# Small linears with standing weights and streaming tokens, four modulation rows in another linear, and later sines

## The reference, cut to what matters

```python
# odd layer
qkv, g, a_in, b_in = split_cols(a @ w_in, ODD_SPLITS)      # a_in and b_in: 16 columns each
log_a = -jnp.exp(a_log) * jax.nn.softplus(a_in + dt_bias)
beta = jax.nn.sigmoid(b_in)
# hybrid layer: columns for the indexer's head weights (8) and for the gates of the mLSTM (4 and 4)
IN_SPLITS = (Q_RANK, ATT_WIDTH, ATT_WIDTH, IDX_DIM, N_IDX_HEADS,
             MLSTM_WIDTH, MLSTM_WIDTH, MLSTM_WIDTH, MLSTM_WIDTH, MLSTM_HEADS, MLSTM_HEADS)
cos, sin = jnp.cos(ang), jnp.sin(ang)                      # rotary tables from the positions
```

## Time and profile before

| | |
|---|---|
| time, median of 3 runs | 2228.63 us (2227.8 to 2230.28) |
| the profiled execution | 2229.53 us, span 2227.8 us |
| mean granted clock of TensorE | 0.943 |
| PE busy | 2048.6 us, 92% |
| DVE busy | 1507.7 us, 68% |
| ACT busy | 901.8 us, 40% |
| POOL busy | 140.4 us, 6% |
| HBM read | 320.84 MB, 144 GB/s over the span |

### The profile page before, as it was taken

How to read it: one execution, slowest core, us unless ns; L and a number is a source line. 1 busy time by engine, 2 the same in 40 slices (tenths; PEclk the granted TensorE clock), 3 DMA queues, 4 the chain that set the end, 5 groups by cost and what they waited for, 6 DMA issues and landing times. The chain is left out here.

```text
span 2227.8 us, 40146 instructions
## 1 busy us (share of the span) xinstructions
PE 2048.6 (92%) x16858; PEld 1831.8 (82%) x16858; DVE 1507.7 (68%) x2320; ACT 901.8 (40%) x1338; POOL 140.4 (6%) x231
## 2 busy tenths in 40 slices
PE   6998987999999799899988999798899989988997
PEld 5786865788888588688886999698799979887997
DVE  6866566998676758656646777768666666956454
ACT  3436443222222433322325444546444355554443
POOL 0100000011000011201210000000000000000000
PEclk7999989999999889899998999899899999988999
DMA  8532022455553366100003777343357734323552
GB/s 329 200 125 76 1 95 95 176 184 190 187 187 115 117 227 221 45 3 3 3 21 114 256 276 277 106 145 102 125 207 276 275 111 155 130 95 111 181 183 92
DMA packets 59133, 323.94 MB, mean 145 GB/s; under 512 B 6384, under 2 KB 7536, under 8 KB 32624
## 3 DMA queue, kind: packets, MB, share of 16 engines
q1 hardware_dynamic: 33360, 228.97, 29.2%
q0 software_dynamic: 25344, 92.29, 11.8%
q10 hardware_dynamic: 288, 0.66, 0.1%
HBM read 320.84 MB, written 1.05 MB: 144 GB/s over the span
## 5 line engine op out<-in xcount | busy, mean ns | idle before, releaser
L370 DVE TENSOR_TENSOR w_low<-raw,w_high 128x1024 fp32r<-128x1024 f32 (+1 forms) x408 | 473.4, 1202 | 243.5 <-ACT w_high L362 243.2
L362 ACT ACTIVATE w_high<-raw 128x1024 fp32r<-128x1024 f32 (+1 forms) x408 | 402.5, 1035 | 397.6 <-PE banks L407 389.2
L548 DVE SCALAR_TENSOR_TENSOR mod_rows<-mod_rows,silu_condition 128x1024 f32<-128x1024 f32 x176 | 212.9, 1221 | 14.3 <-DMA mod_rows<-rows_dram 11.7
L405 PE MATMUL banks<-ffn_a_l,w_high 128*128 128x256 f32 x704 | 199.7, 284 | 1.9 <-DVE ffn_hidden L1006 1.9
L406 PE MATMUL banks<-ffn_a_h,w_high 128*128 128x256 f32 x704 | 199.1, 283 | 0.0
L407 PE MATMUL banks<-ffn_a_h,w_low 128*128 128x256 f32 x704 | 199.1, 283 | 0.0
L405 PE MATMUL banks<-mlp_a_l,w_high 128*128 128x512 f32 (+1 forms) x512 | 176.7, 345 | 11.9 <-DVE mlp_a_l L690 7.7
L534 POOL DMA_DIRECT2D mod_rows<-rows_dram x176 | 93.2, 530 | 1368.4 <-DVE mod_rows L548 1152.1
L406 PE MATMUL banks<-mlp_a_h,w_high 128*128 128x512 f32 (+1 forms) x512 | 175.2, 342 | 0.0
L407 PE MATMUL banks<-mlp_a_h,w_low 128*128 128x512 f32 (+1 forms) x512 | 174.9, 342 | 0.0
L405 PE MATMUL banks<-mlp_hidden_l,w_high 128*128 128x512 f32 (+1 forms) x512 | 173.3, 338 | 1.3 <-DVE mlp_hidden_l L1014 1.3
(11 more groups left out here) (598 smaller groups left out, 4876.4 us busy)
## 6 DMA issues: line engine op xcount, KB each, us to landing
raw<-panels_dram SPq DMA_DIRECT2D x204, 1024.0 KB, 4.8
mod_rows<-rows_dram POOLq DMA_DIRECT2D x176, 512.0 KB, 5.1
mod_0a_rows<-rows_dram SPq DMA_DIRECT2D x8, 1024.0 KB, 19.4
x_features<-x_features_dram SPq DMA_DIRECT2D x1, 2048.0 KB, 11.3
constants<-small_dram SPq DMA_DIRECT2D x1, 1672.5 KB, 6.8
silu_condition<-conditions_dram SPq DMA_DIRECT2D x2, 512.0 KB, 12.5
out_dram<-x_features SPq DMA_DIRECT2D x4, 256.0 KB, 2.1
constants<-small_dram SPq DMA_DIRECT2D x1, 736.5 KB, 5.4
```

Of the source, the lines that this page charges most:

```text
L362: self.nc.scalar.activation(self.wh[:, m % 2, cols], self.raw[:, slot, cols], ACT.Copy).then_inc(self.w_high, 1)
L370: self.nc.vector.tensor_tensor(self.wl[:, m % 2, cols], self.raw[:, slot, cols], self.wh[:, m % 2, cols].bitcast(F32), ALU.subtract).then_ ...
L405: self.nc.tensor.matmul(out, sh(k), ml(k), start=(opens and k == 0), stop=False)
L548: nc.vector.scalar_tensor_tensor(row if v == nv - 1 else self.scratch[:], row, 1.0, self.cond[v][:], ALU.mult, ALU.mult, accum_out=mod[:, ...
```

## The change

It does five things.

1. `odd_ab_in` becomes one block: the 32 weight columns are stationary (`narrow`) and all 512 tokens stream, 24 products into one bank of 32 partitions. ACT copies it to `pre[0:32, 7, :]`. At panel 1 of `odd_v` PE transposes it in four pieces into bank 7 (`turn_narrow`), and the gate inputs read it from there.
2. `mix_small_in` of both hybrid layers does the same with 256 tokens: 24 products, an ACT copy to `work`, two transposes at panel 0 of `mix_v_in` behind the rotation products, and an ACT copy to `sm`.
3. The gates of the hybrid layers move: the 4 small DVE operations behind the rotary work at `mix_v_in` panel 0, exp and ln to panel 1 behind the relus, the last two DVE operations to the first panel of `mix_rest`.
4. The two Sin activations move from ahead of `mix_in`'s copies into `mix_small_in`, behind ACT's split of the next panel.
5. The rows: `odd_g` takes 1, 1, 2 and 2 and `odd_ab_in` none (6 where there were 10); `odd_out` takes one per panel. `linear` now carries the free marks of the prior linear's banks on.

```diff
@@ -802,7 +802,8 @@
-            info.update(done=done, taken=taken, bank_free=bank_free)
+            kept = prior["bank_free"] if prior is not None else {}
+            info.update(done=done, taken=taken, bank_free={**kept, **bank_free})
@@ -862,6 +863,22 @@
         return product
+
+    def narrow(self, high, low, n, width, nk):
+
+        def product(q, m, bank):
+            return self.product3(bank[0:width, 0:n],
+                                 lambda k: self.wh[:, m % 2, k * width:(k + 1) * width],
+                                 lambda k: self.wl[:, m % 2, k * width:(k + 1) * width],
+                                 lambda k: high[:, k, 0:n], lambda k: low[:, k, 0:n], nk)
+        return product
+
+    def turn_narrow(self, pe, src, out, width):
+
+        for i in range(src.shape[1] // P):
+            last = self.nc.tensor.transpose(out[:, i * width:(i + 1) * width], src[:, i * P:(i + 1) * P],
+                                            self.c("ident")[0:width, 0:width])
+        return last
@@ -1719,7 +1736,7 @@
-    ab = pr.sb("odd_ab", [P, 4, 32], ctx=inner)
+    ab = ps[:, 7, 0:P].rearrange("p (i n) -> p i n", n=32)
@@ -1746,10 +1763,16 @@
                         pr.copy_out(lambda q: gate[:, q, :]), a_ready, info=g_info, rising=True,
-                        beside=lambda which, eng, p: beside(which, eng, 2))
-    ab_ready = pr.linear("odd_ab_in", 1, 4, 4, pr.tokens(high, low, 4, 32, KD),
-                         pr.copy_out(lambda q: ab[:, q, :]), [], prior=g_info, info=ab_info,
-                         beside=lambda which, eng, p: beside(which, eng, 2))
+                        beside=lambda which, eng, p: beside(which, eng, 1 + p // 2))
+    ab_ready = pr.linear("odd_ab_in", 1, 1, 1, pr.narrow(high, low, N, 32, KD),
+                         lambda q, which, eng, bank: nc.scalar.activation(pre[0:32, 7, :], bank[0:32, :], ACT.Copy), [],
+                         engines=("act",), prior=g_info, info=ab_info)
+    ab_turned = pr.sem("odd_ab_turned")
+
+    def turn_ab(pe):
+        for w in ab_ready:
+            pe.wait_ge(*w)
+        pr.turn_narrow(pe, pre[0:32, 7, :], ps[:, 7, 0:P], 32).then_inc(ab_turned, 1)
@@ -1769,8 +1792,7 @@
-        for w in ab_ready:
-            dve.wait_ge(*w)
+        dve.wait_ge(ab_turned, 1)
@@ -1818,7 +1840,8 @@
-    gate_steps = {("dve", 1): gate_inputs, ("act", 1): gate_logs, ("dve", 2): log_decays}
+    gate_steps = {("dve", 1): gate_inputs, ("act", 1): gate_logs, ("dve", 2): log_decays,
+                  ("pe", 1): turn_ab}
@@ -2524,12 +2547,11 @@
-        @pr.block.scalar
-        def _(act):
-            act.wait_ge(angles_ready, 2)
-            nc.scalar.activation(sin[:], sin[:], ACT.Sin).then_inc(ready, 1)
-            nc.scalar.activation(cos[:], cos[:], ACT.Sin).then_inc(ready, 1)
-    return [(ready, 2)]
+    def sines(act):
+        act.wait_ge(angles_ready, 2)
+        nc.scalar.activation(sin[:], sin[:], ACT.Sin).then_inc(ready, 1)
+        nc.scalar.activation(cos[:], cos[:], ACT.Sin).then_inc(ready, 1)
+    return sines, [(ready, 2)]
@@ -2656,21 +2678,23 @@
               engines=who[:8], rising=True, beside=beside_first, info=a_info, first_out=conv_first(0))
-    pr.linear("mix_small_in", 1, 2, 2, pr.tokens(high, low, 2, 32, KD), pr.copy_out(lambda q: sm[:, q, :]), [],
-              engines=("act",), prior=a_info, info=sm_info)
-
-    def beside_q(which, eng, p):
-        if which == "dve":
-            eng.wait_ge(*sm_info["taken"][1])
-            b = lambda name: spread(c(name)[:, 4 * l:4 * l + 4], 1, 2)
-            nc.vector.tensor_tensor(ig, sm[:, :, 8:12], b("b_ig"), ALU.add)
-            nc.vector.tensor_scalar(w_idx[:], sm[:, :, 0:8], (8 * 64) ** -0.5, None, ALU.mult)
-            ch.then(eng, nc.vector.tensor_tensor(lf, sm[:, :, 12:16], b("b_fg"), ALU.add))
-            nc.vector.scalar_tensor_tensor(tmp, lf, -1.0, lf, ALU.mult, ALU.max).then_inc(gates_abs, 1)
+    sm_t = work[0:32, 0, :]
+    pr.linear("mix_small_in", 1, 1, 1, pr.narrow(high, low, N, 32, KD),
+              lambda q, which, eng, bank: nc.scalar.activation(sm_t, bank[0:32, 0:N], ACT.Copy), [],
+              engines=("act",), prior=a_info, info=sm_info,
+              beside=lambda which, eng, p: sines(eng) if which == "act" else None)
+    sm_turned, sm_out = pr.sem("mix_small_turned"), pr.sem("mix_small_tokens")
+
+    def gate_inputs(dve):
+        dve.wait_ge(sm_out, 1)
+        b = lambda name: spread(c(name)[:, 4 * l:4 * l + 4], 1, 2)
+        nc.vector.tensor_tensor(ig, sm[:, :, 8:12], b("b_ig"), ALU.add)
+        nc.vector.tensor_scalar(w_idx[:], sm[:, :, 0:8], (8 * 64) ** -0.5, None, ALU.mult)
+        ch.then(dve, nc.vector.tensor_tensor(lf, sm[:, :, 12:16], b("b_fg"), ALU.add))
+        nc.vector.scalar_tensor_tensor(tmp, lf, -1.0, lf, ALU.mult, ALU.max).then_inc(gates_abs, 1)
     pr.linear("mix_q_up", 1, 8, 8, pr.features(cq_h, cq_l, N, 2, lambda q, k: (q * 2 + k) * P),
-              pr.copy_out(lambda q: qr[:, (q + 4) % 8, :]), [(cq_split, 1)], prior=sm_info, info=q_info,
-              beside=beside_q)
+              pr.copy_out(lambda q: qr[:, (q + 4) % 8, :]), [(cq_split, 1)], prior=sm_info, info=q_info)
@@ -2688,11 +2712,11 @@
             nc.tensor.matmul(ps[:, 6, 0:N], c("rot"), pj[:, KI, :], start=True, stop=True).then_inc(idx_rotated, 1)
+            eng.wait_ge(*sm_info["taken"][0])
+            pr.turn_narrow(eng, sm_t, ps[:, 7, 0:64], 32).then_inc(sm_turned, 1)
         if which == "act" and p == 0:
-            eng.wait_ge(gates_abs, 1)
-            nc.scalar.activation(tmp, tmp, ACT.Exp, scale=-1.0).then_inc(gates_exp, 1)
-            eng.wait_ge(gates_exp, 1)
-            nc.scalar.activation(tmp, tmp, ACT.Ln, bias=1.0).then_inc(gates_log, 1)
+            eng.wait_ge(sm_turned, 1)
+            nc.scalar.activation(flat(sm[:]), ps[:, 7, 0:64], ACT.Copy).then_inc(sm_out, 1)
         if which == "dve" and p == 0:
@@ -2703,8 +2727,10 @@
             nc.vector.tensor_tensor(pj[:, KI, :], pj[:, KI, :], rot[:, 4, :], ALU.add).then_inc(idx_roped, 1)
+            gate_inputs(eng)
         if which == "pe" and p == 1:
             eng.wait_ge(idx_roped, 1)
+            eng.wait_ge(sm_out, 1)
             index_scores(eng, idx_done, range(8), 0, 4)
@@ -2713,10 +2739,10 @@
                                      ACT.Relu).then_inc(idx_relu, 1)
-        if which == "dve" and p == 1:
-            eng.wait_ge(gates_log, 1)
-            ch.then(eng, nc.vector.scalar_tensor_tensor(lf, lf, 0.0, tmp, ALU.min, ALU.subtract))
-            nc.vector.tensor_scalar(nlf, lf, -1.0, None, ALU.mult).then_inc(gates_ready, 1)
+            eng.wait_ge(gates_abs, 1)
+            nc.scalar.activation(tmp, tmp, ACT.Exp, scale=-1.0).then_inc(gates_exp, 1)
+            eng.wait_ge(gates_exp, 1)
+            nc.scalar.activation(tmp, tmp, ACT.Ln, bias=1.0).then_inc(gates_log, 1)
@@ -2778,6 +2804,9 @@
+            eng.wait_ge(gates_log, 1)
+            ch.then(eng, nc.vector.scalar_tensor_tensor(lf, lf, 0.0, tmp, ALU.min, ALU.subtract))
+            nc.vector.tensor_scalar(nlf, lf, -1.0, None, ALU.mult).then_inc(gates_ready, 1)
@@ -3195,17 +3224,19 @@
-            take, _ = pr.row_work("mod2_0a", [(2 * N_MOD, 34, 1, pr.mod2[0], 0, b_mod[0])], slots, [], silu_ready)
+            take, _ = pr.row_work("mod2_0a", [(2 * N_MOD, 30, 1, pr.mod2[0], 0, b_mod[0])], slots, [], silu_ready)
...
+            take_rest, rest = pr.row_work(
+                "mod2_0b", [(2 * N_MOD + 30, 18, 1, pr.mod2[0], 30, b_mod[0]),
+                            (3 * N_MOD, 16, 1, pr.mod2[1], 0, b_mod[1])], slots, [pr.after_rule], [])
...
-                              pr.add_gated(mod, 16, 1, TL), y_split, engines=("dve",), rising=True)
+                              pr.add_gated(mod, 16, 1, TL), y_split, engines=("dve",), rising=True,
+                              beside=lambda which, eng, p: take_rest(eng, 1) if which == "dve" else None)
...
-            ready = mlp(1, mod, 1, TL, ready, lambda t: pr.row_work(
-                "mod2_0b", [(2 * N_MOD + 34, 14, 1, pr.mod2[0], 34, b_mod[0]),
-                            (3 * N_MOD, 16, 1, pr.mod2[1], 0, b_mod[1])], slots, [pr.after_rule], []), {1: 1, 2: 1})
+            ready = mlp(1, mod, 1, TL, ready, lambda t: (take_rest, rest), {1: 1, 2: 1})
...
```

More of the change, by code:

```diff
@@ L2601, in hybrid_mixer @@
     pr.presplit(2)
-    tables_ready = tables()
+    sines, tables_ready = tables()
     tap = lambda b, n: c("conv_w")[:, l * 32 + n * 8 + b:l * 32 + n * 8 + b + 1]
@@ L3229, in second @@
             take = lambda eng, count: None
-            tables = lambda: []
+            tables = lambda: (lambda act: None, [])
             if l == 0:
```

## The result

| | before | after |
|---|---|---|
| time, median (lowest to highest) | 2228.81 us (2227.80 to 2230.28), 4 runs | 2207.26 us (2203.70 to 2210.05), 4 runs |
| profiled execution, span | 2227.8 us | 2206.2 us |
| mean granted clock | 0.943 | 0.951 |

The medians lie 21.6 us apart. The recorded ratio of the times is 0.9894, with a 95% interval of 0.988 to 0.9909, which is 23.6 us less (20.3 to 26.7). The forecast was 2207, 21.6 less. The sum is met, but not each of its terms, and the rest of this document is mostly about two terms that missed in opposite directions.

The account below looks back on a forecast made before the run. PE was taken to bound nearly everywhere (busy 92%). Savings of 13.5 + 3.8 + 1.1 + 3.3 = 21.7 us from 2229.5 gave 2207.8, median 2207; forecast's own bounds 2205 to 2210, with rivals 2202 to 2214 (about 0.8).

Parts of the forecast that it names:

- Part 1: Odd layer's small linear as 24 products of 512 columns: `odd_v` starts earlier, net 13.5 us saved (11 to 14).
- Rival C: Odd layer: fifth or sixth row lands late, DVE splits `odd_v`'s first panel two to three us late; 2210, chance 0.13.
- rival B: Half clock behind the 32-column stationaries in the odd layer and hybrids, as behind the 32-wide products; 2212, chance 0.10.
- The four moved rows: Rows moved to `odd_out`, one per panel, cost nothing; up to 4 x 1.3 = 5 us if the cover were gone.
- Part 2: First hybrid layer: moving the sines removes PE's 2.11 us hole before the rotation and its half clock; 3.8 us saved (2.0 to 4.0).
- Part 3: Small linear and `q_up` of both hybrid layers: 1.6 and 3.8 us saved, assuming half clock behind the new holes.
- rival A: Clock holds at 2.4 GHz through both hybrid holes ahead of `mix_q_up`; 2.5 us more saved, 2204.5, chance 0.15.
- The gates: Hybrid layers: transposes cost 0.15 us, later DVE operations in `mix_rest` 0.35 a layer, cutting 1.6 and 3.8 to 1.1 and 3.3.
- rival F: Each ACT table switch has a tail of 1.3 us, delaying `q_up`'s bank and `mix_rest`'s first split; about 2211, chance 0.02.

Follow-up runs that it names:

- the fill: Changed kernel plus matrix products nobody reads, 8 ahead of `odd_v` and 15 ahead of `mix_q_up` in both hybrid layers: 2208.59 us, ratio 0.991.
- the odd part alone: Kernel before with only the odd layer's new small linear, its transposes and the moved rows; hybrid layers as before: 2220.08 us, ratio 0.9954.
- the sines earlier: Changed kernel with the two Sin activations and their load moved into ACT's idle time ahead of `mix_in`'s last block: 2205.58 us, ratio 0.9903.
- that with ten rows: Changed kernel with the rows back as before: two per panel of `odd_g`, two in `odd_ab_in`, none in `odd_out`: 2212.09 us, ratio 0.9927.
- that with four rows: Changed kernel with one row per panel in `odd_g`, four in all, and six in `odd_out`: 2206.07 us, ratio 0.9907.

## Why the prediction was right, point by point

**Part 1, 13.5 us: mis-sized by 3.1.** The distance is 10.43 us shorter in the profile, below the 11 to 14 that the step allowed. Two terms missed. The condition of the step was that `odd_v`'s first panel is split in time; the forecast took 797 for it, measured from 791.34, so 5.7 us behind `odd_ab_in`, and gave a late row 0.13. The row was late in three of the five profiles with six rows in `odd_g` (the changed kernel twice, and with the fill; in time in the odd part alone and with the sines earlier), and it cost 1.2 to 2.5 us of start. Rival C named the mechanism and the place; its chance of 0.13 was too low. Its price of 3 us is near the measured 2.8, but for another sum: it took the split to be two to three us late and had no half clock behind the hole, which costs 1.5 to 1.6 us (8 products at 0.43 instead of 0.23). 1.2 + 1.6 are 2.8 of the 3.1; the clean step itself measures 13.2. The rest of the step held: the 24 products 5.7 us (5.5), no half clock among them, which takes rival B out, and ACT's copy 0.59 (0.58 of the 128x512 in the earlier trace rows); transposes 0.43 us (0.5).

**The four moved rows: right.** `odd_out` is 27.12 us after and 27.24 before, and even six rows cost nothing there.

**Part 2, sines, 3.8: right against this profile of before.** 3.84 measured; the chain of the step (ACT free, then DVE's angle chain and `w_low`, no half clock) is seen. With the sines alone PE waits 1.02 us for `w_low` at 1439.59, where the forecast had 1439.5. Of the 3.8, 1.7 was the half clock behind the old hole, and that does not come each time: against the profile of the odd part alone the step is worth 2.4.

**Part 3, 1.6 and 3.8: the mechanism was right, the clock was not.** The first product of `mix_q_up` came 5.11 and 4.69 us behind T0 (forecast 5.3 and 4.7), by the releasers named. The holes were 2.13 and 1.73 us (forecast 2.5 and 1.9), and the second is as long as the 1.72 of the earlier trace rows, behind which the clock had stayed at 1.00. The half clock did not come: the gains are 2.53 and 5.34, which are rival A's 2.5 and 5.4, with its chance of 0.15. The sizes of both readings were sound: 11.64 us to the rotation at full clock (forecast 11.7), and 12.38 in the one profile with half clock there (forecast 12.6). But the gains are counted from one profile of before. Where the old stretch came out at 15.76 and 14.15 us, with nothing edited in it, they would be 4.1 and 3.7, so the agreement of each to 0.1 us is luck of that profile.

**The gates, 0.5 a layer: the wait was right, the whole too dear.** PE's wait for `w_low` in `mix_rest`, 1.25 and 1.23 us before, is 1.51 after in both layers. These are the 0.3 of the step; the stretches that hold them grew by 0.06 and 0.26 only, and the 0.15 for the transposes can't be told from the clock's swings.

**The table load (rival F): out.** The Sin load of 1.28 us ends at 1443.19 and the activation starts at 1443.21. A second time, in the kernel with the sines earlier, 1434.32 and 1434.34. The Trainium skill, page "ScalarE: Activation LUTs", section "What ACT_TABLE_LOAD costs", has 1.38 us of drain on top; neither of these two loads shows it.

**Why the sum came out.** Against the forecast's terms the profile has 3.1 us less in the odd layer, 0.9 and 1.5 more at the two `mix_q_up`, and the gates cost 0.3 over both layers (0.06 and 0.26 in the table) and not 1.0: together nearly zero. The swings of stretches that were not touched (1.04, 0.22, -0.15 and -1.39) sum to -0.3. The forecast was at 2207 for a kernel whose runs lie from 2203.7 to 2210.05, so a part of the closeness is luck.

## What to carry to other kernels

A linear costs PE as many rounds of products as its stationary side has blocks. With the 512 tokens stationary there were four blocks of 128, so 96 products that each streamed only 32 columns; with the 32 columns stationary there is one block, so 24 products that stream 512 tokens, at a granted clock of 1.00 (the old stretch was at 0.64). What bounds next is then whatever the long detour had covered; look for it before moving (here the split of the next panel, a table load, and a row's transfer in DVE's order of work), and move transfers with an uncertain landing out of the order ahead of a split. Count a transfer at its slowest landing in the stretch, not at its mean, when an engine waits for it in line with critical work. And measure the stretch that a change removes in more than one profile of the old kernel: here it swung by 1.6 us with nothing edited, as much as some of the terms.

## What was not expected of the hardware

The granted clock does not follow the length of a hole. Behind holes of 2.13 us at the same place it was 1.00 in the changed kernel's two profiles and in that with ten rows, and 0.54 in that with four rows; behind the hole in front of the sines' rotation 0.50 (2.11 us), 0.54 (2.01 us) and, in the odd part's profile, 1.00 although that hole was 3.32 us:

```profile
1440.30:1444.00 3.70, 3.70 (x18) 3.70 (x19) 2.70 (x3) 2.12 (x3) 0.00 (x0) 0.54 0.82 283
```

(The window of the kernel with four rows, behind the hole of 2.13 us.) What decides it is not known. No half clock was seen behind the holes of 0.77 us in front of `odd_v` and of 1.7 us in front of `mix_q_up`. A forecast should carry a hole of about 2 us with both clocks and not with one. When the half clock came, it cost 1.5 to 1.6 us where PE alone bounded (2.3 behind the hole of 5.09 us), and 0.74 in `mix_q_up`, where a later wait took up the rest.

The same 512 KB row, issued at the same place of the program, landed after 8.5 us in one execution and 5.3 in another, with no edit ahead of it. SP issued the next weight panel 0.6 us behind that row in all five profiles with six rows in `odd_g`. Where the row was late, row and panel landed within 0.4 us of each other (793.81 and 793.98 in the changed kernel); where it was in time, the row landed 1.6 to 1.9 us ahead of the panel (790.28 and 792.14 in the odd part alone). What makes the one or the other is open.
